# Two transformer layers' worth of attention and feed-forward on one core: fewer dummy products at the start, and the last row tile's variance, output and stores cut differently

## The reference, cut to what matters

```python
def block(x, mem, ...):                    # x (1, 512, 1024), all float32
    h = hybrid_mixer(x, ...)               # x @ w_in, three attention branches, gates, output projection
    x = layer_norm(ALPHA * x + h, ln1_g, ln1_b)
    h = memory_cross_attention(x, mem, ...)
    x = layer_norm(ALPHA * x + h, ln2_g, ln2_b)
    a, b = split(x @ w_ffn_in)
    h = (silu(a) * b) @ w_ffn_out
    return layer_norm(ALPHA * x + h, ln3_g, ln3_b)

def layer_norm(x, g, b):
    mu = mean(x, -1)
    var = mean((x - mu) ** 2, -1)
    return (x - mu) * rsqrt(var + 1e-5) * g + b
```

## Time and profile before

| | |
|---|---|
| time, median of 3 runs | 866.27 us (865.78 to 866.29) |
| the profiled execution's own time | 867.16 us |
| its span | 865.2 us |
| TensorE busy | 855.8 us (99%) |
| VectorE busy | 557.4 us (64%) |
| ScalarE busy | 373.3 us (43%) |
| GpSimd busy | 84.5 us (10%) |
| transfers | 90.36 MB, mean 104 GB/s |
| chain of waits that ended last | PE 96% |

### The profile page before, as it was taken

How to read it: one execution, slowest core, us unless ns; L and a number is a source line. 1 busy time by engine, 2 the same in 40 slices (tenths; PEclk the granted TensorE clock), 3 DMA queues, 4 the chain that set the end, 5 groups by cost and what they waited for, 6 DMA issues and landing times.

```text
span 865.2 us, 13234 instructions
## 1 busy us (share of the span) xinstructions
PE 855.8 (99%) x5104; PEld 743.7 (86%) x5104; DVE 557.4 (64%) x1016; ACT 373.3 (43%) x748; POOL 84.5 (10%) x103
## 2 busy tenths in 40 slices
PE   9999999999999999999999999999999999999996
PEld 9988898877678888888889979899999999888885
DVE  5434357778532525262867589689888999877944
ACT  5121167139642222222325545365565566424511
POOL 4100000172200000000000000101211111000000
PEclk9999999999999999999999999999999999999998
DMA  8535532330013222226422311223322233651101
GB/s 292 165 98 146 123 98 72 99 98 2 1 36 99 93 94 93 98 96 237 176 98 90 106 50 50 98 80 114 101 98 98 99 100 121 264 197 49 49 25 73
DMA packets 72951, 90.36 MB, mean 104 GB/s; under 512 B 3298, under 2 KB 63478, under 8 KB 72894
## 3 DMA queue, kind: packets, MB, share of 16 engines
q1 hardware_dynamic: 72510, 89.15, 30.9%
q0 software_dynamic: 384, 0.43, 0.3%
HBM read 87.05 MB, written 2.52 MB: 104 GB/s over the span
## 4 chain that ended last, share of the span: by engine, by line
PE 96%; DVE 1%; issue 1%; ACT 0%; POOL 0%; DVEq 0%; POOLq 0%; ACTq 0%
PE ps L2400 19%; PE ps L2402 19%; PE ps L2401 19%; PE ps L2935 7%; PE ps L2934 7%; PE ps L2933 7%; PE ps L2526 3%; PE ps L2603 3%; PE ps L2563 3%; PE ps L2991 1%; PE ps L2993 1%; PE ps L2992 1%; PE ps L2437 1%; PE ps L3036 1%; PE ps L3037 1%
## 5 line engine op out<-in xcount | busy, mean ns | idle before, releaser
L2400 PE MATMUL ps<-xt_hi,w_hi 128*128 128x512 f32 (+1 forms) x400 | 155.4, 389 | 0.0
L2402 PE MATMUL ps<-xt_lo,w_hi 128*128 128x512 f32 (+1 forms) x400 | 154.8, 387 | 0.0
L2401 PE MATMUL ps<-xt_hi,w_lo 128*128 128x512 f32 (+1 forms) x400 | 154.8, 387 | 0.0
L1138 ACT CAST w_hi<-raw 128x1024 fp32r<-128x1024 f32 (+1 forms) x48 | 49.4, 1034 | 134.2 <-PE ps L2402 113.8
L1899 DVE TENSOR_TENSOR w_lo<-raw,w_hi 128x1024 fp32r<-128x1024 f32 x30 | 36.7, 1224 | 90.1 <-ACT w_hi L1302 90.1
L2400 PEld LDWEIGHTS ps<-xt_hi,w_hi 128*128 128x128 f32 x400 | 75.1, 188 | 15.7 <-issue 0.6
L2402 PEld LDWEIGHTS ps<-xt_lo,w_hi 128*128 128x128 f32 x400 | 75.1, 188 | 15.3
L2401 PEld LDWEIGHTS ps<-xt_hi,w_lo 128*128 128x128 f32 x400 | 75.1, 188 | 15.1
L2935 PE MATMUL ps<-xt_lo,w_hi 128*128 128x256 f32 x288 | 81.5, 283 | 0.0
L2934 PE MATMUL ps<-xt_hi,w_lo 128*128 128x256 f32 x288 | 81.5, 283 | 0.0
L2933 PE MATMUL ps<-xt_hi,w_hi 128*128 128x256 f32 x288 | 81.5, 283 | 0.0
(11 more groups left out here) (384 smaller groups left out, 1974.9 us busy)
## 6 DMA issues: line engine op xcount, KB each, us to landing
raw<-in_w_in SPq DMA_DIRECT2D x24, 1024.0 KB, 4.8
raw<-in_w_ffn_in SPq DMA_DIRECT2D x36, 512.0 KB, 4.4
raw<-in_w_ffn_out SPq DMA_DIRECT2D x7, 1024.0 KB, 4.7
raw<-in_w_mix_out SPq DMA_DIRECT2D x4, 1024.0 KB, 5.0
raw<-in_w_ffn_in SPq DMA_DIRECT2D x4, 1024.0 KB, 5.4
out_w<-in_w_ffn_out SPq DMA_DIRECT2D x4, 1024.0 KB, 8.1
raw<-in_w_branch_b SPq DMA_DIRECT2D x4, 512.0 KB, 3.7
resid<-in_x SPq DMA_DIRECT2D x1, 2048.0 KB, 9.7
```

The costliest lines, as they stand in the source:

```text
L1138: act.copy(hi, src).then_inc(hi_done, 1)
L2400: pe.matmul(dst, a_hi, b_hi, start=start, stop=False, skip_group_check=reopened)
L2401: pe.matmul(dst, a_lo, b_hi, start=False, stop=False, skip_group_check=reopened)
L2402: return pe.matmul(dst, a_hi, b_lo, start=False, stop=stop, skip_group_check=reopened)
```

## The change

- `keep_warm(12)` becomes `keep_warm(7)`.
- The last tile's squares are taken half by half about minus the mean of the left half alone (`neg_left`), whose row sum is known before the right half is there. ScalarE makes the left half's square, 1/1024 of its sum plus the epsilon (`last_var[0]`), then the right half's square, and the variance from it with `last_var[1]` as the addend. GpSimd supplies that addend: the gap between the two means, its square, and `last_var[0]` minus it, since the mean square about any value is the variance plus the square of that value's distance from the mean.
- The last tile's output is made in pieces of 512, 256 and 256 columns, each with its store.

```diff
+        LAST_COLS = (slice(0, 512), slice(512, 768), slice(768, 1024))
...
-            for c in range(2):
+            for c, cols in enumerate(LAST_COLS):
                 sp.wait_ge(norm_done, 3 * TT + c)
-                cols = slice(512 * c, 512 * c + 512)
                 sp.dma_start(out[0, (TT - 1) * P:, cols], resid[:, TT - 1, cols]).then_inc(stored, 16)
-            sp.wait_ge(stored, 16 * (TT + 1))
+            sp.wait_ge(stored, 16 * (TT - 1 + len(LAST_COLS)))
...
+                if n == 3 * TT - 1:
+                    pool.wait_ge(mean_done, n + 1)
+                    pool.tensor_tensor(mean_gap[:, 0:1], neg_mean[:, t:t + 1], neg_left[:, 0:1], ALU.subtract).then_inc(gap_step, 1)
+                    pool.wait_ge(gap_step, 1)
+                    pool.tensor_tensor(mean_gap[:, 1:2], mean_gap[:, 0:1], mean_gap[:, 0:1], ALU.mult).then_inc(gap_step, 1)
+                    pool.wait_ge(gap_step, 2)
+                    pool.wait_ge(left_var_done, 1)
+                    pool.tensor_tensor(last_var[:, 1:2], last_var[:, 0:1], mean_gap[:, 1:2], ALU.subtract).then_inc(gap_step, 1)
                 pool.wait_ge(var_done, n + 1)
                 pool.tensor_tensor(rstd[:, t:t + 1], var[:, t:t + 1], half[:, 0:1], ALU.pow).then_inc(rstd_done, 1)
...
-            for t in range(TT):
+            for t in range(TT - 1):
                 square(2 * TT + t)
+            act.wait_ge(neg_left_done, 1)
+            for c in range(2):
+                cols = slice(512 * c, 512 * c + 512)
+                act.wait_ge(y_done, 2 * (3 * TT - 1) + c + 1)
+                act.activation(squares[:, cols], resid[:, TT - 1, cols], ACT.Square, bias=neg_left[:, 0:1],
+                               accum_out=last_sq[:, c:c + 1]).then_inc(last_sq_done, 1)
+                if c == 0:
+                    act.wait_ge(last_sq_done, 1)
+                    act.activation(last_var[:, 0:1], last_sq[:, 0:1], ACT.Copy, scale=1.0 / D, bias=LN_EPS).then_inc(left_var_done, 1)
+            act.wait_ge(last_sq_done, 2)
+            act.wait_ge(gap_step, 3)
+            act.activation(var[:, TT - 1:TT], last_sq[:, 1:2], ACT.Identity, scale=1.0 / D,
+                           bias=last_var[:, 1:2]).then_inc(var_done, 1)
...
-                link(dve.scalar_tensor_tensor(out=sa[:, :, :].rearrange("p a c -> p (a c)"), in0=resid[:, t, :],
-                                              scalar=neg_mean[:, t:t + 1], in1=gb[:, 0, :], op0=ALU.add, op1=ALU.mult))
-                dve.wait_ge(sq_done, n + 1)
+                dve.scalar_tensor_tensor(out=sa[:, :, :].rearrange("p a c -> p (a c)"), in0=resid[:, t, :],
+                                         scalar=neg_mean[:, t:t + 1], in1=gb[:, 0, :], op0=ALU.add,
+                                         op1=ALU.mult).then_inc(dve_step, 1)
+                dve.wait_ge(last_sq_done, 2)
                 dve.wait_ge(rstd_done, n + 1)
...
-            for t in range(TT):
+            for t in range(TT - 1):
                 norm_sums(2 * TT + t)
...
+                norm_out(2 * TT + t)
+            norm_sums(3 * TT - 1, (0,))
+            dve.wait_ge(y_done, 2 * (3 * TT - 1) + 1)
+            dve.tensor_scalar(neg_left[:, 0:1], row_sum[:, TT - 1, 0:1], -2.0 / D, None, ALU.mult).then_inc(neg_left_done, 1)
+            norm_sums(3 * TT - 1, (1,))
+            dve.wait_ge(mean_done, 3 * TT)
+            norm_last(3 * TT - 1)
...
-            keep_warm(12)
+            keep_warm(7)
```

More of the change, by code:

```diff
@@ L389, in build_layer @@
         row_sum = sb("row_sum", [P, TT, 2])
+        neg_left = sb("neg_left", [P, 1])
+        last_sq = sb("last_sq", [P, 2])
+        last_var = sb("last_var", [P, 2])
+        mean_gap = sb("mean_gap", [P, 2])
         neg_mean = sb("neg_mean", [P, TT])
@@ L571, in build_layer @@
         stored = sem("stored")
+        neg_left_done, last_sq_done, left_var_done, gap_step = (
+            sem("neg_left_done"), sem("last_sq_done"), sem("left_var_done"), sem("gap_step"))
         def stat_col(kind, h, t):
@@ L1966, in norm_last @@
                 t = n % TT
-                link(dve.scalar_tensor_tensor(out=sa[:, :, :].rearrange("p a c -> p (a c)"), in0=resid[:, t, :],
-                                              scalar=neg_mean[:, t:t + 1], in1=gb[:, 0, :], op0=ALU.add, op1=ALU.mult))
-                dve.wait_ge(sq_done, n + 1)
+                dve.scalar_tensor_tensor(out=sa[:, :, :].rearrange("p a c -> p (a c)"), in0=resid[:, t, :],
+                                         scalar=neg_mean[:, t:t + 1], in1=gb[:, 0, :], op0=ALU.add,
+                                         op1=ALU.mult).then_inc(dve_step, 1)
+                dve.wait_ge(last_sq_done, 2)
                 dve.wait_ge(rstd_done, n + 1)
-                for c in range(2):
-                    cols = slice(512 * c, 512 * c + 512)
-                    dve.scalar_tensor_tensor(out=resid[:, t, cols], in0=sa[:, c, :], scalar=rstd[:, t:t + 1], in1=gb[:, 1, cols],
+                chain[0] += 1
+                dve.wait_ge(dve_step, chain[0])
+                for cols in LAST_COLS:
+                    dve.scalar_tensor_tensor(out=resid[:, t, cols], in0=sa[:, :, :].rearrange("p a c -> p (a c)")[:, cols],
+                                             scalar=rstd[:, t:t + 1], in1=gb[:, 1, cols],
                                              op0=ALU.mult, op1=ALU.add).then_inc(norm_done, 1)
```

## The result

The changed kernel takes **868.62 us** (median of 8 runs, 868.34 to 869.19) beside 866.4 for the kernel before in the same comparison (8 runs, 865.78 to 867.21): ratio 1.0025, 95% interval 1.0016 to 1.0035. It is 2.2 us slower. The forecast was 865.9 in a range of 864.0 to 866.8: wrong in sign and outside its range.

The account below looks back on a forecast made before the run. The prediction took TensorE's products to bound nearly the whole span, so only the two ends could change the time. Front -1.06, tail +0.74 and stores 0 gave -0.32, so 865.9 us from a median of 866.27, range 864.0 to 866.8.

Parts of the forecast that it names:

- the sentence on the front: Start: no transfer stops TensorE and later loads and casts wait for it, so the earlier start reaches the end.
- my slower one: Rival at the start: fewer dummies and a short gap put off the clock's rise; at 13 us +2.2, 868.4; chance 0.04.
- the sum: The forecast's addition of front, tail and stores: -1.06 + 0.74 + 0 = -0.32 us.
- The front, -1.06: Start: products begin 1.87 earlier, at 5.2; slow-clock products lose 1.03 against 0.22 before; ends -2.09 and -0.9.
- my single row: Start: the one clock rise on record, at about 7.5 us, on which the front's -1.06 rests.
- the rival that drew on it: Start: the clock is up before 5.2, front term -2.09, total -1.35, 864.9; chance 0.20.
- The tail, +0.74: Tail: GpSimd's first small operation is held until VectorE's sa ends, so the final products start 0.74 later; upper end +1.77.
- The rival that GpSimd isn't held: Tail: GpSimd's three operations run beside sa unheld, variance starts 0.33 earlier, total -1.4, 864.9; chance 0.15.
- The stores, 0: End: three pieces drain back to back, last store issued 0.12 later with half the bytes; 0, ends -0.1 and +0.12.
- The rule by which this term would have been -0.18: Final stores: a DMA costs about 2.0 us plus bytes over 436 GB/s, so 128 KB less saves 0.3, issue 0.12 later.

Follow-up runs that it names:

- run 1: The kernel before with one unused buffer of 128 bytes per partition ahead of neg_mean: 869.4 us, ratio 1.0034.
- run 2: The whole change with its four small buffers laid inside the existing pad_base, so no other buffer moves: 866.14 us, ratio 0.9997 to the kernel before.
- run 5: The kernel before with 32 unused bytes per partition ahead of neg_mean: 869.08 us, ratio 1.0027.
- run 6: The kernel before with pad_base 128 bytes longer, so every buffer, w and xt too, lies 128 bytes higher: 866.94 us beside 866.96.
- run 7: The kernel before with 256 unused bytes per partition ahead of neg_mean: 866.65 us beside 866.75.
- Run 8: The kernel of run 2, with VectorE's product into sa waiting for GpSimd's three small operations: 866.2 us, one run.
- run 3: The kernel before with 7 dummy products instead of 12, nothing else: 866.1 us, ratio 0.9993.
- run 4: The kernel before with its last half row made and stored in two pieces, nothing else: 867.08 us, ratio 1.0006.

## Why the prediction was wrong, point by point

**The step that failed** is the sentence on the front, "No transfer binds, and later loads and casts wait for TensorE, so the shift travels to the end." It takes for granted that between the two ends each product costs what it cost. The middle became 2.98 longer, and no rival had it: my slower one was a late rise of the clock. The declarations of four small buffers had no price in the sum. They are in the diff, `w_hi` stands above them in the list of buffers and `h_hi` below, and the list has buffers named `pad_base` and `pad_line` that nothing uses, a sign that places had been chosen. Runs 1 and 2 show what these four lines cost: 2.6 in run 1's middle, and 2.5 between the medians of the change with and without the shift (868.62 and 866.14). Runs 5 to 7 show what about them costs it.

**The size of it.** Some 650 to 670 products by 6 to 6.5 ns are about 4.2, yet the middle of run 1 grew by 2.56. The other 1.7 comes back in products of 256 columns, some 1980 of them, each 0.85 ns shorter. ScalarE's casts show it in the feed-forward's first product, where TensorE has products of 256 columns alone, 168 between these two rows. Before:

```profile
690.28 0.62 ACT L1414 CAST w_hi<-raw 128x512 fp32r<-128x512 f32 x1
...
710.44 0.62 ACT L1414 CAST w_hi<-raw 128x512 fp32r<-128x512 f32 x1
```

and in run 1:

```profile
690.55 0.62 ACT L1415 CAST w_hi<-raw 128x512 fp32r<-128x512 f32 x1
...
710.55 0.62 ACT L1415 CAST w_hi<-raw 128x512 fp32r<-128x512 f32 x1
```

20.16 and 20.00. The same shift slows one shape and slightly helps the other. It helps also where both operands stayed in place (xt with w, by some 0.7 ns); why is open, so the rule of the two operands isn't the whole account of this shape. The changed kernel's middle is 0.41 longer than run 1's. Its trace has a late transfer that run 1's has not, near 637 us:

```profile
636.89 0.62 ACT L1429 CAST w_hi<-raw 128x512 fp32r<-128x512 f32 x1 [0.65 <-DMA raw<-in_w_ffn_in]
```

At 638.4 TensorE then takes 0.32 longer than usual from one product to the next, the most of the 0.41. The late transfer recurs without the shift. Run 8 has it (and 0.20 at 637.4)

```profile
635.80 0.62 ACT L1426 CAST w_hi<-raw 128x512 fp32r<-128x512 f32 x1 [0.56 <-DMA raw<-in_w_ffn_in]
```

and run 2, with the same buffers, has not; their middles are 839.79 and 839.45. So it comes and goes with the execution. The profiled execution's span is 867.2, while six of the eight have 866.4 to 866.9.

**The front, -1.06: the mechanism right, the size within reach.** No operand was late. In run 3's chain the products start at 4.97, where the sum had 5.2: 2.10 earlier than before. The slow stretch costs 2.09 + 1.17 - 2 x 0.94 = 1.38, where the sum had 1.03, against 0.22 before; -2.10 + 1.38 - 0.22 is the -0.94 measured. The clock rose when the sum had it. In run 3's trace the single products start 0.43 apart up to 7.29, then 0.31, then 0.24; in that of before 0.30 apart from 7.30 on, then 0.24. So in both it rose between 7.3 and 7.6. Of the 0.35 over the sum's 1.03, 0.1 is the earlier start (0.23 x 0.45) and 0.2 the first product, from which it is 0.61 to the second in every kernel with 7 or 2 dummies, against 0.43 from one to the next behind it at the lower clock; the sum had no such term. In the changed kernel, with 7 dummies too, the starts from 5.02 on are 0.61, 0.27 and 0.23 apart: the clock rose between 5.6 and 5.9. Four slow products fewer, of 0.19 each, make the 0.76 between -0.94 and -1.70. That the moment differs with nothing changed ahead of it is shown by the kernels that kept all 24 passes, which take 5.49 before and in run 6, 5.38 in run 1, 5.00 in run 7, 4.75 in run 4 and 4.30 in run 5:

```profile
1.58 4.30 PE ps L2449 x24
5.88 1.06 PE ps L2457 x4
```

So the rule of the Trainium skill that I had set against my single row ("TensorE: Matmul & The Clock Gate", Part 1, the transition isn't tied to the kernel's start) is borne out, and the rival that drew on it was nearer in this trace (-2.09 for the measured -1.70), by the luck of one execution. But its end of -2.09 counted wrongly: when the clock rises early the dummies of the kernel before are shorter as well, and an execution of before gains with it. The medians, over many rises, give the 5 dummies -0.4 (run 3, interval -1.4 to +0.3).

**The tail, +0.74: measured +0.52** from `neg_mean` to the final products (3.01 against 2.49), by almost the predicted way. GpSimd's chain ended last and `sa` did hold it. But it was the second small operation that was held (1.05, ending 0.06 behind `sa`'s 861.73), not the first: the first began 0.05 after `sa` and took 0.19. Each is 0.19 alone. The variance takes 0.29 with an addend from memory, where I had put 0.20. (The Trainium skill, in "ScalarE: Activation LUTs", What ACT_TABLE_LOAD costs, has each such operand add about 93 ns; the rows agree.) The rival that GpSimd isn't held falls; the statement of the Trainium skill ("GPSIMD Engine Reference", 1. Specifications, the table) that GpSimd contends with VectorE instructions that have two inputs in SBUF agrees with these rows, which add how much.

**The stores, 0: measured +0.1** (run 4, from the final products to the end; 0.1 to 0.2 in the changed kernel). The final products of 512, 256 and 256 columns take 1.54 for 1.41, about the 0.12 that I had as the upper end. The stores drained without a break, as the earlier trace rows did. The engines of the changed kernel, at the same distance from the final products:

```profile
864.80:866.20 1.40, 0.00 (x0) 0.00 (x0) 0.00 (x0) 0.00 (x0) 0.00 (x0) 0.50 1.00 353
```

The rule by which this term would have been -0.18, in "DMA: Bandwidth & Descriptors", Anatomy of one DMA, of the Trainium skill (there for GpSimd's queue), is not borne out for a store behind another: 128 KB less in the last one gave nothing.

**The sum again.** With -0.94, +0.52, +0.1 and the middle's +2.56 it is +2.2, and the medians differ by 2.2. That they agree so well is in part luck, as the -0.94 holds for a late rise of the clock. From medians alone, run 1's +2.9 and run 2's -0.4, it is +2.5, which the intervals allow.

## What to carry to other kernels

Where TensorE is busy for 99% of the time, a change of 0.006 us in a product's pace is worth more than anything at either end, and no wait shows it: compare first how far apart the same products start in both traces, stage by stage. A new buffer, however small, is part of a change: declare it inside a buffer that is there (run 2), or behind all operands of products, which wasn't tried here. A disputed slowdown can be tested by a dead buffer of that size alone. Small operations for GpSimd don't belong beside a large VectorE product of two inputs.

## What the runs showed of the hardware that was not expected

- A TensorE product of 512 columns in this float32 form starts every 227 ns or, on average, every 233 ns, depending on where its two operands lie in SBUF relative to each other. Moving one by 32 or 128 bytes costs 6.5 ns a product (runs 5 and 1), moving one by 256 or everything by 128 costs nothing (runs 7 and 6). What makes it so isn't shown. Over the kernel, 2.1 to 2.9 us.
- A product of 256 columns goes the other way, from 120.0 to 119.2 ns on average (runs 1 and 5, and the changed kernel), cause open.
- The clock reached its upper level at moments that differ by some 3 us between executions, read from the distances of products: with 7 dummies between 5.6 and 5.9 in the changed kernel and between 7.3 and 7.6 in run 3; with 12 between 7.3 and 7.6 before and in run 5 during the dummies, whose passes start 0.21 apart up to 4.3 and 0.11 from 4.5 on. With 2 dummies it was the latest, between 8.8 and 9.2, in the one execution seen.
- A GpSimd operation on one column beside a VectorE product with two SBUF inputs took 1.05 instead of 0.19 (0.55 became 1.35 for the power), unless it began 0.05 us after that product's start (0.19, in the changed kernel and in run 2).
